# Encoder layer on one core: attention's norms in pieces, memory scaled on GpSimd, two turns moved, half-width products

## The reference, cut to what matters

```python
def hybrid_mixer(hn, ...):              # mq mk mv mo mg hq hff hfb hi hg fu nq nk nv = split(hn @ w_in)
    qk = silu(centred_dwconv(concat([mq, mk]), conv_w))
    y_ml = sigmoid(mo) * merge_heads(h_fwd + h_bwd)          # mLSTM over q, k, v, gates
    o = o * rsqrt(mean(o * o, axis=-1) + EPS)                # HGRN2, per head
    y_hg = merge_heads(o) * silu(hg)
    y_fn = fft2(u).real ; y_na = neighbourhood_attention(nq, nk, nv, rpb)
    y = rms_norm(stack([y_ml, y_hg, y_fn, y_na]), group_gain)   # each group of 512 by itself
    return y @ w_out

def reference(x, mem, ...):
    mem_n = rms_norm(mem, norm_mem)
    h = x + hybrid_mixer(rms_norm(x, norm_mix), ...)
    h = h + memory_cross_attention(rms_norm(h, norm_cross), mem_n, xa_wq, xa_wk, xa_wv, xa_wo)
    h = h + hierarchical_moe(rms_norm(h, norm_ffn), ...)    # 2 of 32 experts for each token
    return rms_norm(h, norm_final)
```

## Time and profile before

| | |
|---|---|
| median of 3 runs | 1905.98 us (1905.55 to 1908.88) |
| profiled execution | 1907.17 us, its span 1905.3 us |
| busy, share of the span | PE 93%, DVE 44%, ACT 27%, POOL 2% |
| granted TensorE clock, mean | 0.962 |
| chain that ended last | PE 71%, DMA 22%, DVE 4%, ACT 2%, issue 1% |
| DMA | 560.98 MB, of which the experts' weights are more than 400 MB |

### The profile page before, as it was taken

One profiled execution on the slowest core, in us unless ns is written; L12 is line 12 of the kernel. 1 busy time (PEld: TensorE's weight loads), 2 busy tenths in 40 slices (PEclk: granted clock), 3 DMA queues, 4 the chain that ended last, 5 costly groups with the idle time before them and its releaser, 6 DMA issues.

```text
span 1905.3 us, 24767 instructions
## 1 busy us (share of the span) xinstructions
PE 1769.2 (93%) x10056; PEld 1127.0 (59%) x10056; DVE 834.2 (44%) x1181; ACT 523.2 (27%) x756; POOL 41.5 (2%) x25
## 2 busy tenths in 40 slices
PE   7989999999798999999799989899899899899996
PEld 7889899799677789988644323233333333333332
DVE  5655555798554654344553323323233233232233
ACT  5353443644334444343420100100000001000002
POOL 0000000032000000000000000000000000000000
PEclk9999999999899999999899989999899899999998
DMA  8653645444344565527489999999999999999995
GB/s 325 241 177 119 206 160 171 144 148 144 119 149 161 176 200 169 170 75 264 199 339 417 428 427 428 429 428 429 414 430 428 428 429 429 429 428 428 428 428 236
DMA packets 105389, 560.98 MB, mean 294 GB/s; under 512 B 9696, under 2 KB 9824, under 8 KB 79200
## 3 DMA queue, kind: packets, MB, share of 16 engines
q1 hardware_dynamic: 95808, 436.13, 58.7%
q10 hardware_dynamic: 9504, 123.74, 15.4%
HBM read 557.75 MB, written 2.10 MB: 294 GB/s over the span
## 4 chain that ended last, share of the span: by engine, by line
PE 71%; DMA 22%; DVE 4%; ACT 2%; issue 1%; SPq 0%; ACTq 0%; DVEq 0%
DMA arena<-in_moe_w_dram 21%; PE ps L952 16%; PE ps L605 6%; PE ps L599 6%; PE ps L600 6%; PE ps L601 6%; PE ps L606 6%; PE ps L607 6%; PE ps L980 6%; PE ps L963 3%; PE ps L997 2%; DVE w_lo L1540 1%; PE ps L898 1%; PE ps L841 1%; PE ps L822 1%
## 5 line engine op out<-in xcount | busy, mean ns | idle before, releaser
L952 PE MATMUL ps<-arena 128*64 128x512 f32 x2048 | 499.4, 621 | 59.1 <-DMA arena<-in_moe_w_dram 57.4
L1540 DVE TENSOR_TENSOR w_lo<-arena,w_hi 128x1024 fp32r<-128x1024 f32 x264 | 318.2, 1247 | 263.6 <-ACT w_hi L1121 263.4
L1121 ACT ACTIVATE w_hi<-arena 128x1024 fp32r<-128x1024 f32 x264 | 264.6, 1051 | 311.1 <-PE ps L601 168.8
L952 PEld LDWEIGHTS ps<-arena 128*64 128x64 f32 x2048 | 136.1, 140 | 319.0 <-issue 247.4
L2137 DVE TENSOR_TENSOR arena<-ps,arena 128x1024 f32<-128x1024 f32 x128 | 156.7, 1225 | 241.9 <-PE ps L997 241.9
L980 PE MATMUL ps<-arena 128*64 128x512 f32 x1024 | 227.5, 597 | 2.4 <-DVE arena L2114 1.8
L599 PE MATMUL ps<-x_hi,w_hi 128*128 128x256 f32 x512 | 148.2, 289 | 16.7 <-DVE w_lo L1540 16.7
L980 PEld LDWEIGHTS ps<-arena 128*64 128x64 f32 x1024 | 73.6, 138 | 149.5 <-issue 145.5
L600 PE MATMUL ps<-x_lo,w_hi 128*128 128x256 f32 x512 | 147.1, 287 | 0.0
L601 PE MATMUL ps<-x_hi,w_lo 128*128 128x256 f32 x512 | 147.1, 287 | 0.0
L2131 DVE TENSOR_TENSOR d_lo<-ps,d_hi 128x512 fp32r<-128x512 f32 x64 | 41.2, 686 | 236.9 <-ACT d_hi L1411 236.9
(11 more groups left out here) (363 smaller groups left out, 2542.1 us busy)
## 6 DMA issues: line engine op xcount, KB each, us to landing
arena<-in_moe_w_dram SPq DMA_DIRECT2D x133, 2048.0 KB, 19.4
arena<-in_moe_w_dram ACTq DMA_DIRECT2D x58, 2048.0 KB, 14.0
arena<-in_w_in_dram SPq DMA_DIRECT2D x52, 1024.0 KB, 5.1
arena<-in_xa_wk_dram SPq DMA_DIRECT2D x16, 1024.0 KB, 5.1
arena<-in_xa_wv_dram SPq DMA_DIRECT2D x16, 1024.0 KB, 5.0
arena<-in_w_out_dram SPq DMA_DIRECT2D x16, 1024.0 KB, 5.0
arena<-in_xa_wq_dram SPq DMA_DIRECT2D x16, 1024.0 KB, 5.0
arena<-in_xa_wo_dram SPq DMA_DIRECT2D x16, 1024.0 KB, 5.1
```

The costliest lines, as they stand in the source:

```text
L952: last = mm(ps[rows_, m, :], xe[par][:, ECH * i + c, :], ring_up[m][i][:, c, :], start=(i == 0 and c < 2), stop=(i == ECH - 1 and c >= 2))
L1121: fn(hi_ring[(2 * n + u) % 4][:], ring_a[i][:, 2 * u:2 * u + 2, :], ACT.Copy).then_inc(S["w_hi"], 1)
L1540: V.tensor_tensor(w_lo[i][:, 2 * u:2 * u + 2, :], ring_a[i][:, 2 * u:2 * u + 2, :], hi_ring[(2 * n + u) % 4][:].bitcast(F32), ALU.subtract ...
```

## The change

Six parts, with some of the diff left out where lines only follow.

```diff
@@ gpsimd: the memory's scaling, ahead of HGRN2's steps (was DVE's, in beside(4))
+            pool.wait_ge(S["rms_row"], 2)
+            for n in range(NCH):
+                at = mem_t[:, CH * n:CH * (n + 1), :]
+                nc.gpsimd.tensor_tensor(at, at, bc_mid(mem_rms, CH), ALU.mult).then_inc(S["m_rows"], 1)
+            for n in range(NCH):
+                at = mem_t[:, CH * n:CH * (n + 1), :]
+                pool.wait_ge(S["m_rows"], n + 1)
+                nc.gpsimd.tensor_tensor(at, at, bc_last(cols[:, 3 * KT + CH * n:3 * KT + CH * (n + 1)], T), ALU.mult).then_inc(S["m_gain"], 1)
@@ scalar: its high half beside group 11 and at the start of group 12's block
+            def memory_hi(part):
+                for n in part:
+                    act.wait_ge(S["m_gain"], n + 1)
+                    fn(split["mem"][0][:, CH * n:CH * (n + 1), :], mem_t[:, CH * n:CH * (n + 1), :], ACT.Copy).then_inc(S["m_hi"], 1)
+                if g == G_IN - 2:
+                    act.wait_ge(S["ml_y"], NH)
+                    memory_hi((0, 1))
                 if g == G_IN - 1:
+                    memory_hi((2, 3))
                     act.wait_ge(S["fn_pe"], 1)
...
-                    act.wait_ge(S["m_dve"], 1)
-                    by_gain(mem_t, split["mem"][0], 3, range(KT // 2), "m_hi")
                     high(g, (3,))
...
-                    by_gain(mem_t, split["mem"][0], 3, range(KT // 2, KT), "m_hi")
@@ vector, group 12
                     V.tensor_tensor(yml, yml, buf["mo"], ALU.mult).then_inc(S["yv_mo"], 1)
+                    memory_lo((0, 1, 2))
                     dve.wait_ge(S["fn_pe"], 1)
...
                     low(g, (2,))
+                    dve.wait_ge(S["yv_mo"], 1)
+                    memory_lo((3,))
...
-                    by_gain_low(mem_t, split["mem"], 3, range(KT // 2), "m_hi", "m_lo")
@@ vector, beside: q after group 1, k after group 2
-                if g == 1:
+                if g in (1, 2):
                     dve.wait_ge(S["proj_b"], 2)
-                    for n, (raw, dst) in enumerate((("mq", "q"), ("mk", "k"))):
+                    n, (raw, dst) = g - 1, (("mq", "q"), ("mk", "k"))[g - 1]
@@ scalar, beside
                     fn(flat(buf["q"]), flat(buf["q"]), ACT.Silu).then_inc(S["silu_act"], 1)
+                if g == 3:
                     act.wait_ge(S["conv_dve"], 2)
                     fn(flat(buf["k"]), flat(buf["k"]), ACT.Silu).then_inc(S["silu_act"], 1)
@@ vector, attention's blocks, behind the row maxima
                 V.tensor_scalar(st[:, 52:54], st[:, 52:54], -1.0, None, ALU.mult).then_inc(S["na_max"], 1)
+                if m == 1:
+                    head_squares()
+                if m == 2:
+                    head_norm()
+                if m == 3:
+                    group_squares(1)
+                if m == 4:
+                    group_norm(1)
                 for c in NA_CHUNKS[m][1:]:
                     low_of(KT + c)
...
-                if m == 0:
-                    second_norm()
-                if m == 1:
-                    group_norm(1)
@@ scalar, end of a block
-                if m < 2:
-                    rsqrt(NT * NH if m == 0 else NT)
+                if m in (1, 3):
+                    rsqrt(NT * NH if m == 1 else NT)
+                    exp_table()
@@ tensor, last block of attention, and the turns
+HALVES = (slice(0, 64), slice(64, 128))
+TURN_BANK = (4, 7, 5, 6)
                 chunk_of_wv(NA_CHUNKS[m][1:])
+                if m == NA_H // 2 * NT - 1:
+                    pe.wait_ge(S["y_done"], 3)
+                    turn_split(0, y, part=(0, 1))
                 pe.wait_ge(S["na_tev"], m + 1)
...
-                        last = mm(bank(6, 2, NA_D)[:, u, :], npt[:, u, s, :], buf["nv"][...],
-                                  start=(s == 0), stop=(s == NT - 1))
+                        for own in HALVES:
+                            last = mm(bank(6, 2, NA_D)[own, u, :], npt[:, u, s, own], buf["nv"][...],
+                                      start=(s == 0), stop=(s == NT - 1))
...
-            pe.wait_ge(S["y_done"], 3)
+            turn_split(0, y, part=(2,))
             pe.wait_ge(S["na_y"], 16)
-            turn_split(0, y, part=range(4))
+            turn_split(0, y, part=(3,))
```

More of the change, by code:

```diff
@@ L717, in _ @@
             last_in(3)
+            for c in range(HG_LEAD):
+                pe.wait_ge(S["m_lo"], c + 1)
+                dense_split(G_WK, True, split["mem"], part=[c])
             pe.wait_ge(S["m_lo"], NCH)
-            for c in range(HG_LEAD):
-                dense_split(G_WK, True, split["mem"], part=[c])
             pe.wait_ge(S["hp_dve"], 3)
@@ L887, in _ @@
             o_ = bank(7, 3, NE)
-            mm(o_[:, 0, :], before, hit[:, 0, :], start=True, stop=True)
-            mm(o_[:, 1, :], before, hit[:, 1, :], start=True, stop=False)
-            mm(o_[:, 1, :], ones, hit[:, 0, :], start=False, stop=True)
-            mm(o_[:, 2, :], ones, hit[:, 0, :], start=True, stop=False)
-            mm(o_[:, 2, :], ones, hit[:, 1, :], start=False, stop=True).then_inc(S["r_pe"], 1)
+            for at, left, j, first, done in ((0, before, 0, True, True), (1, before, 1, True, False), (1, ones, 0, False, True),
+                                             (2, ones, 0, True, False), (2, ones, 1, False, True)):
+                for own in HALVES:
+                    last = mm(o_[own, at, :], left[:, own], hit[:, j, :], start=first, stop=done)
+            last.then_inc(S["r_pe"], 1)
             def gather(half, k, at, lo):
@@ L1291, in _ @@
             high(G_WO, (0,))
-            turned_hi(0, split[G_WO][0], 4, part=range(4))
+            turned_hi(0, split[G_WO][0], 4, part=(2, 3))
             high(G_WO, (1,))
+            sqrt_table()
+            rsqrt(NT)
             turned_hi(0, split[G_WO][0], 4, part=(4, 5))
-            rsqrt(NT)
             high(G_WO, (2,))
@@ L1733, in _ @@
                     log_decay(0)
-                    by_gain_low(mem_t, split["mem"], 3, range(KT // 2, KT), "m_hi", "m_lo")
                     low(G_WK, (0,))
```

108 lines of the change are left out of this document (65 added, 43 removed).

## The result

The changed kernel took 1873.39 us (median of 4 runs, 1873.1 to 1874.95) against 1906.84 for the one before (4 runs, 1905.55 to 1908.88): a ratio of 0.9827 with a 95% interval of 0.9815 to 0.9839, so 33 us faster. Forecast were 1878.0 us and a gain of 28.

A forecast was written before the change was run, and what follows sets the result against it. Experts were taken as bound by the weight stream, the dense half by PE and what it waits for. Terms from -16.2 (attention) to +3.0 (GpSimd) summed to -28.1 us, giving 1878.0 us as median; range 1869 to 1888.

The forecast's parts named there:

- What bounds it: Whole kernel: experts bound by the weight stream, the dense half by PE; a microsecond saved before about 990 us counts.
- Convolutions, memory's halves, norms: Stalls at 85 to 95 us, 345 to 357 us and attention's blocks 1 and 2 go: -4.0, -6.0, -16.2.
- GpSimd: Around group 4, its eight products take turns with DVE's low halves and delay PE: +3.0, bounds 0 and +4.5.
- some four more lose 0.8 each: Group 4's low halves beside GpSimd: after the first two, four come late by 0.8 us each; 4.5 at most in all.
- The output matrix: End of attention: half of y's turns and y_lo leave the path, and the 1.24 us norm wait goes: -3.4.
- Half-width products: Eight full products as 16 halves save 0.5 us: router -1.5, ranks -0.2, `sums` -0.4 and -0.4, values 0.
- the first ones: Experts' `sums`: of 32 experts the first ones count -0.4, the last -0.4; the rest is hidden.
- The values at 0: Attention's eight blocks: half-width values gain some 0.2 each, but PE mostly waits for others: 0, bounds 0 to -2.
- Dearer pieces: Rival 1: norm pieces and GpSimd bite harder, attention -8, memory's halves -3.5, group 4 +1.5 more; 1890 us, chance 0.17.
- Halves as dear as whole ones: Rival 2: two half-width products cost as much as two full ones in values, router and `sums`; 1894 us, chance 0.05.
- A stream that does not wait: Rival 3: the experts' 830 us start at a fixed time, so only the last expert's 0.4 us shows; 1905.5, chance 0.02.
- GpSimd as a brake of 5.6 us or more a product: Rival 4: GpSimd holds DVE off much longer, a loss from 5.6 us; at 6.5 us a product 1913, chance 0.03.

## Why the prediction was right

The time lies 4.6 us below the forecast and inside the range (1869 to 1888); what bounds the kernel was read rightly. By its steps:

- **What bounds it.** A saving ahead of the experts came through whole: -31.6 us at `up`, -33.7 at the end. The stream's rate is as before (428 GB/s), and PE's wait for it grew in its place.
- **Convolutions, memory's halves, norms:** -4.3, -6.5 and -16.7 in the trace against -4.0, -6.0 and -16.2. Putting the first two back one at a time brought back stops of 2.67 and 2.16 us, putting the norms back cost 16.2 us. The stall is the size of the gain when the work that caused it has slack at its new place.
- **GpSimd.** The mechanism, taking turns, was right and the size was not: +3.0 was forecast, 1.0 was the first half's lateness, and PE had no stop after it. The term that was mis-sized is "some four more lose 0.8 each", which rests on "a half in 2.5 + 1.2 = 3.7 us" for all eight. Only three halves came at such a pace (3.38 to 3.43 us), beginning in the slow clock behind PE's stop; the second four products are shorter (2.87 us), and a half took 2.91 beside them, just PE's 2.9. That the whole stretch came out at +3.0 for a forecast of +4.0 is luck. Besides 1.0 for GpSimd and 0.96 for the Silu (as forecast) it has a clock of 0.87 from 163 to 176 us, 1.5 us, which was not foreseen, and 0.6 us gained back, since less of the slow clock near 140 us lay behind the later restart.
- **The output matrix:** -4.1 for -3.4, of which the turns 2.07 (forecast 2.1); the rest was not tested by itself.
- **Half-width products.** The router's 0.55 us a group was right. `sums` was mis-sized twice: a group of eight products saves 1.0 us and not 0.5, and "the first ones" are those until PE's first wait for weights, at 1055 us here and at 1089 with whole products. Together -2.1 in place of -0.8, and +2.9 when put back alone. The values at 0 were wrong too: 1.0 us in attention, since nothing covers PE's products once its waits are gone. The ranks' -0.2 came out as +0.2 up to `up`: whole ranks cost 0.3 more when put back, but the last router group ran at half clock in the changed kernel, and its 32 half rows took 1.93 us for 1.95 of 16 whole ones at full clock. The row that the price of a whole product came from (1.79 us) also moves 128 columns where the one of 1.08 moves 64; `sums`, with 64, shows that this made little difference (1.93).
- **The rest.** The clock's toss is 1.6 us. The base was 0.9 us low (1905.98 for 1906.84), which hid part of the miss: the gain is 5.3 us over its forecast, the time only 4.6 under.
- **The rivals.** Dearer pieces: attention came out at the forecast's size. Halves as dear as whole ones: a half row took 0.03 us and a whole one 0.12. The rule of the Trainium skill ("TensorEngine Tiling (Array Packing)", Instruction Overhead), that a product has about 60 cycles of overhead and a small dimension should not be cut, did not bring this rival about. What was cut are 128 columns of weights, not the small side (64 moving columns in `sums` and the values, 36 in the router), and by an estimate from that figure at 2.4 GHz the overhead is 0.025 us, which fits into the 0.03 of a half. A stream that does not wait: SP's waits are unchanged and the end came 33 us sooner. GpSimd as a brake of 5.6 us or more a product: no half took longer than 3.43. But turns of 2.9 us were enough to cost 7 us by the landmarks, 8.8 by the medians, when the same eight products started 48 us later. That the change's place had cover for them is in part luck.

## What to carry to other kernels

Ask of each stop which engine's queue the late work stands in, and whether what stands ahead of it is needed soon; here 27 of 33 us came from work that only had to go behind something, and a stall plus the slow clock behind it gave the size. Work moved to GpSimd is not free to DVE: in these rows each low half, which reads both inputs from SBUF, then waits for one GpSimd operation. That cost 1 us where PE takes its work at that pace and 7 to 9 us where DVE's result was already late; short operations were the better neighbours. When stops go, price again what they covered.

## What the runs showed that I had not expected

- The 16 small products of the gates that begin at 164.23 us (1.94 us together) were followed by a fall of the clock (0.87 from 163 to 176 us) in the changed kernel and in ten of its twelve variants; in the kernel before, in the one without GpSimd, and in the one with both the Silu moved and GpSimd late it stayed at 1.00. PE was busy all 13 us in the changed kernel, and GpSimd was at rest there. What decides it stays open.
- A row with 64 columns of weights took 0.03 us where one with 128 took 0.12: two halves cost half of a whole.
- A stop of the same length is followed by the half clock in some executions and not in others, worth 1.5 us at 805 us and about as much at 88 us. Below 2 us the median of five runs tells less than the distance between two landmarks of the trace.
